# Sigmoids of the second merge in other batches, first squares on two engines, a root table asked for early, weight splits ahead of waiting rows

## The reference

```
first block:  h = rms_norm(x); proj = h @ w_in
              gated linear attention (4 heads, chunks of 64), a width-3 causal convolution branch
              merged = sigmoid(g_a)*y_a + sigmoid(g_c)*y_c;  x += merged @ w_out
              x += sigmoid(rms_norm(x) @ w_ple_gate) * (p @ w_ple_proj);  x = rms_norm(x)
second block: z = rms_norm(x) @ w_in_2
              y_a = mlstm(z) @ w_up_a       (4 heads, forward and backward, chunks of 128)
              y_b = diff_attention(z) @ w_up_b   (4 heads, softmax pairs, ALiBi bias)
              x += (sigmoid(z[gate 0])*y_a + sigmoid(z[gate 1])*y_b) @ w_out
              h2 = rms_norm(x); aff = softmax(h2 @ w_router)    (16 experts)
              each expert takes its 64 best tokens: silu(xe@w_gate)*(xe@w_up) @ w_down, times aff
              out = rms_norm(x + sum of the experts' rows)
```

## Time and profile before

| | |
|---|---|
| runs before | 1989.58, 1990.76, 1990.95 us, median 1990.76 |
| the profiled execution | 1988.47 us, span 1986.7 us |
| mean granted PE clock | 0.988 |
| PE busy | 1890.8 us (95%), 8735 matmuls |
| DVE / ACT / POOL busy | 728.8 / 520.7 / 68.8 us |
| DMA | 504.93 MB, 432 to 434 GB/s in nearly all of the second half |
| chain that ended last, by share | PE 66%, DMA 23%, issue 7%, ACT 2%, DVE 1%, POOL 1% |

### The profile page before, as it was taken

The page is one execution under the profiler, slowest core; times in us unless marked ns, Lnnn a source line. Parts: engine busy times, 40 slices in busy tenths (PEclk is TensorE's granted clock), DMA queues, the critical chain, the costliest instruction groups (busy, mean ns, idle before and its releaser), DMA issues.

```text
span 1986.7 us, 20688 instructions
## 1 busy us (share of the span) xinstructions
PE 1890.8 (95%) x8735; PEld 1147.6 (58%) x8735; DVE 728.8 (37%) x1213; ACT 520.7 (26%) x839; POOL 68.8 (3%) x62
## 2 busy tenths in 40 slices
PE   8999999999999999999997999999898998999998
PEld 6788888888887888876874333333233333333332
DVE  6544444333356764786353111111111110111112
ACT  5444323222345343277532000000000000000002
POOL 2000000000014001100020000000000000000000
PEclk9999999999999999999998999999999999999999
DMA  5221322322323232121377999999999999999997
GB/s 188 85 85 64 117 95 96 98 100 100 106 89 106 74 128 107 64 64 43 113 313 302 421 427 432 432 434 432 432 433 432 432 432 432 432 433 432 433 428 297
DMA packets 49324, 504.93 MB, mean 254 GB/s; under 512 B 6416, under 2 KB 7440, under 8 KB 30544
## 3 DMA queue, kind: packets, MB, share of 16 engines
q1 hardware_dynamic: 48368, 502.49, 62.0%
q10 hardware_dynamic: 864, 1.12, 0.2%
HBM read 499.39 MB, written 4.19 MB: 253 GB/s over the span
## 4 chain that ended last, share of the span: by engine, by line
PE 66%; DMA 23%; issue 7%; ACT 2%; DVE 1%; POOL 1%; SPq 0%; ACTq 0%; POOLq 0%; DVEq 0%
PE ps L2107 35%; DMA ring_a<-in_experts_in 22%; PE ps L2463 10%; PE ps L2474 6%; PE ps L2042 4%; PE ps L2422 3%; PE ps L2446 1%; PE ps L2509 1%; POOL xacc L785 1%; POOL gbl L819 0%; ACT hidT L1237 0%; DMA x_in<-in_xT_in 0%; PE ps L2485 0%; PE ps L2227 0%; PE ps L2210 0%
## 5 line engine op out<-in xcount | busy, mean ns | idle before, releaser
L2463 PE MATMUL ps<-ring_a,xe 128*64 128x512 f32 x1504 | 342.8, 609 | 43.6 <-DMA ring_a<-in_experts_in 43.0
L2463 PEld LDWEIGHTS ps<-ring_a,xe 128*64 128x64 f32 x1504 | 107.0, 140 | 273.3 <-issue 211.9
L1282 DVE TENSOR_TENSOR d_lo<-d_raw,d_hi 128x1024 fp32r<-128x1024 f32 x166 | 208.3, 1263 | 123.8 <-ACT d_hi L851 123.1
L2107 PE MATMUL ps<-n_hi,d_hi 128*128 128x512 f32 x448 | 176.0, 393 | 1.5 <-DVE d_lo L1282 0.8
L2107 PE MATMUL ps<-n_lo,d_hi 128*128 128x512 f32 x448 | 174.5, 389 | 0.0
L2107 PE MATMUL ps<-n_hi,d_lo 128*128 128x512 f32 x448 | 174.4, 389 | 0.0
L851 ACT ACTIVATE d_hi<-d_raw 128x1024 fp32r<-128x1024 f32 x166 | 170.9, 1049 | 9.3 <-DMA d_raw<-in_tiles_in 7.6
L1512 DVE TENSOR_TENSOR hid<-hid,ps 128x512 f32<-128x512 f32 x32 | 20.6, 683 | 411.8 <-PE ps L2463 385.4
L1950 DVE TENSOR_TENSOR acc<-acc,ps 128x1024 f32<-128x1024 f32 x56 | 64.6, 1214 | 242.6 <-PE ps L2446 242.6
L2474 PE MATMUL ps<-ring_a,hidT 128*64 128x512 f32 x648 | 145.7, 596 | 7.5 <-DMA ring_a<-in_experts_in 4.3
L2463 PE MATMUL ps<-ring_b,xe 128*64 128x512 f32 x464 | 103.1, 594 | 3.3 <-DMA ring_b<-in_experts_in 3.3
(11 more groups left out here) (503 smaller groups left out, 2730.2 us busy)
## 6 DMA issues: line engine op xcount, KB each, us to landing
ring_a<-in_experts_in SPq DMA_DIRECT2D x56, 4096.0 KB, 42.0
ring_b<-in_experts_in SPq DMA_DIRECT2D x28, 3072.0 KB, 42.5
d_raw<-in_tiles_in SPq DMA_DIRECT2D x166, 512.0 KB, 3.3
ring_a<-in_experts_in SPq DMA_DIRECT2D x31, 1024.0 KB, 13.0
ring_a<-in_experts_in SPq DMA_DIRECT2D x12, 2048.0 KB, 13.8
ring_b<-in_experts_in SPq DMA_DIRECT2D x5, 2048.0 KB, 13.9
ring_b<-in_experts_in SPq DMA_DIRECT2D x8, 1024.0 KB, 16.7
x_in<-in_xT_in SPq DMA_DIRECT2D x4, 512.0 KB, 6.8
```

The lines of the kernel that those rows point to most:

```text
L1282: dve.tensor_tensor(d_lo[:, n % SLOTS, :, :], d_raw[:, n % SLOTS, :, :], d_hi[:, n % SLOTS, :, :].bitcast(F32), ALU.subtract).then_inc(t_l ...
L2107: mm = pe.matmul(bank, lt[:, n, gr.k0 + k, :], rt[:, k, :], start=k == 0 and m == 0, stop=k == gr.nk - 1 and m == 2)
L2463: mm = pe.matmul(ps[half * CAP:(half + 1) * CAP, 2 * m + q, :], xe[:, k, :], slot(e, n)[:, (2 * q + half) * S:(2 * q + half + 1) * S], sta ...
```

## The change

Nothing of what is computed changes, except the order in which the first eight squares are added. There are five edits.

1. The sigmoids of g2a: n = 0, 1 go into `mlstm_norm` at ("g2a", 3), behind the sigmoid of `moT`; n = 2 to 7 stand in one batch at ("g2a", 7); the batch at ("ua", 2) is gone.
2. At ("g2b", 7) ACT splits the tile after `hd_hi` and before the eight sigmoids; before, it split it ahead of both.
3. In the ub groups ACT splits the tile first and then waits for the row of the merge.
4. POOL adds squares 0 to 3 only; DVE adds 4 to 7 and then both sums, between the early splits. PE waits for DVE.
5. The root table is asked for ahead of the wait for the logits, and the DMA of the triangle is issued behind the root.

```diff
@@ -491,8 +491,8 @@
         set_act = Steps(sem("setup_act"), ["warm", "root"])
         set_dve = Steps(sem("setup_dve"), ["gf2", "gks", "mgs"])
         u_act = Steps(sem("mix_act"), [f"hi{k}" for k in range(KD)] + [f"sq{k}" for k in range(KD)] + ["root"])
-        u_dve = Steps(sem("mix_dve"), [f"lo{k}" for k in range(KD)] + ["R"])
-        u_pool = Steps(sem("mix_pool"), [f"sum{k}" for k in range(1, KD)])
+        u_dve = Steps(sem("mix_dve"), [f"lo{k}" for k in range(KD)] + [f"sum{k}" for k in range(5, KD)] + ["sum", "R"])
+        u_pool = Steps(sem("mix_pool"), [f"sum{k}" for k in range(1, 4)])
         u_pe = Steps(sem("mix_pe"), ["sum"])
         h_dve = Steps(sem("normed_dve"), [n for k in range(KD) for n in (f"h{k}", f"lo{k}")])
         h_act = Steps(sem("normed_act"), [f"hi{k}" for k in range(KD)])
@@ -777,7 +777,7 @@
             pool.wait_ge(set_pool.sem, set_pool.count("reset1"))
             set_pool.done(pool.memset(reset[:, 0:S:GCH], 0.0), "reset")
 
-            for k in range(1, KD):
+            for k in range(1, 4):
                 pool.wait_ge(u_act.sem, u_act.count(f"sq{k}"))
                 if k > 1:
                     pool.wait_ge(u_pool.sem, u_pool.count(f"sum{k - 1}"))
@@ -926,6 +926,11 @@
                 act.wait_ge(mq_dve.sem, mq_dve.count("c4", n))
                 mq_act.done(act.activation(mqkT[:, n, :], scr[1 + n % 2][:, 0:S], ACT.Silu, bias=vcol("cb2", n)), "silu")
 
+            def splits(gr):
+                for n in range(len(TILES)):
+                    if SPLIT[n] == gr.g:
+                        split1(n)
+
             def after(gr):
                 name, i = gr.name, gr.i
                 if name == "gate":
@@ -1046,6 +1051,9 @@
                 biases(0)
                 read_done(act, "mo", MH - 1)
                 f_act.done(act.activation(moT[:, :, :], moT[:, :, :], ACT.Sigmoid), "sig")
+                for n in range(2):
+                    read_done(act, "g2a", n)
+                    sa_act.done(act.activation(graw[:, n, :], graw[:, n, :], ACT.Sigmoid), f"s{n}")
 
             def mlstm_out(h):
                 act.wait_ge(f_t.sem, f_t.count("t", h))
@@ -1160,12 +1168,12 @@
                         mlstm_out(k - FIRST_F)
                     if 0 <= k - FIRST_D < ND + 5:
                         attention(k - FIRST_D)
-                if (name, i) in (("g2a", KD - 1), ("ua", 2)):
-                    for n in range(4) if name == "g2a" else range(4, KD):
+                if (name, i) == ("g2a", KD - 1):
+                    for n in range(2, KD):
                         read_done(act, "g2a", n)
-                        x = graw[:, n, :] if n < 2 else glog(n)
-                        sa_act.done(act.activation(x, x, ACT.Sigmoid), f"s{n}")
+                        sa_act.done(act.activation(glog(n), glog(n), ACT.Sigmoid), f"s{n}")
                 elif (name, i) == ("g2b", KD - 1):
+                    splits(gr)
                     for n in range(KD):
                         read_done(act, "g2b", n)
                         sb_act.done(act.activation(gbl[:, n, :], gbl[:, n, :], ACT.Sigmoid), f"s{n}")
@@ -1190,10 +1198,11 @@
             act.wait_ge(set_pool.sem, set_pool.count("eps"))
             u_act.done(act.activation(R[:, :], ps[:, 7, :], ACT.Sqrt, bias=eps[:, :], scale=1.0 / D), "root")
             for gr in STREAM:
+                if gr.name == "ub":
+                    splits(gr)
                 evict(gr)
-                for n in range(len(TILES)):
-                    if SPLIT[n] == gr.g:
-                        split1(n)
+                if gr.name != "ub" and (gr.name, gr.i) != ("g2b", KD - 1):
+                    splits(gr)
                 if (gr.name, gr.i) == ("dq", 3):
                     gate_logs()
                 if gr.name in ("q", "k"):
@@ -1207,11 +1216,11 @@
                     p_act.done(act.activation(pT_hi[:, k, :], pT_raw[:, k, :], ACT.Copy), f"hi{k}")
                 chain(gr.name, gr.i)
 
-            act.wait_ge(t_dve.sem, t_dve.count("raw"))
-            act.dma_start(tri_raw[:, :], tri_in[:, :]).then_inc(s_tri, 16)
             act.wait_ge(set_act.sem, set_act.count("warm"))
             set_act.done(act.activation(warm[:, :], eps[:, :], ACT.Sqrt), "root")
+            act.wait_ge(t_dve.sem, t_dve.count("raw"))
             t_act.done(act.activation(esm[:, 4:8], lraw[:, :, NE], ACT.Sqrt, bias=eps[:, :], scale=1 / D), "root")
+            act.dma_start(tri_raw[:, :], tri_in[:, :]).then_inc(s_tri, 16)
             act.wait_ge(t_dve.sem, t_dve.count("lg"))
             t_act.done(act.activation(lg[:, :, :], lg[:, :, :], ACT.Exp), "exp")
             for t, b in enumerate((0, 4, 6, 0)):
@@ -1848,7 +1857,18 @@
                 dve.wait_ge(u_act.sem, u_act.count(f"hi{k}"))
                 u_dve.done(dve.scalar_tensor_tensor(out=u_lo[:, k, :], in0=x_in[:, k, :], scalar=vcol("mix", k),
                                                     in1=u_hi[:, k, :].bitcast(F32), op0=ALU.mult, op1=ALU.subtract), f"lo{k}")
-            for n in pre[1:]:
+            for n in pre[1:3]:
+                split1(n)
+            for k in range(5, KD):
+                dve.wait_ge(u_act.sem, u_act.count(f"sq{k}"))
+                if k > 5:
+                    dve.wait_ge(u_dve.sem, u_dve.count(f"sum{k - 1}"))
+                u_dve.done(dve.tensor_tensor(xsq[:, 4, :], xsq[:, 4, :], xsq[:, k, :], ALU.add), f"sum{k}")
+            for n in pre[3:]:
+                if n == pre[4]:
+                    dve.wait_ge(u_pool.sem, u_pool.count("sum3"))
+                    dve.wait_ge(u_dve.sem, u_dve.count(f"sum{KD - 1}"))
+                    u_dve.done(dve.tensor_tensor(xacc[:, :], xacc[:, :], xsq[:, 4, :], ALU.add), "sum")
                 split1(n)
             dve.wait_ge(s_table, 16)
             dve.wait_ge(u_pe.sem, u_pe.count("sum"))
@@ -2297,7 +2317,7 @@
 
             def chain(name, i):
                 if (name, i) == ("q", 2):
-                    pe.wait_ge(u_pool.sem, u_pool.count(f"sum{KD - 1}"))
+                    pe.wait_ge(u_dve.sem, u_dve.count("sum"))
                     u_pe.done(pe.matmul(ps[:, 7, :], ones[:, :], xacc[:, :], start=True, stop=True), "sum")
                 elif (name, i) == ("v", 0):
                     gates_wide()
```

## The result

The changed kernel takes 1977.82 us in the median (1977.08 to 1978.91, 6 runs) against 1989.06 (1988.4 to 1990.95, 6 runs) for the kernel before on the same chip: ratio 0.9944, 95% interval 0.9934 to 0.9954, or 11.2 us faster. The forecast was 1979.3, the sum of the terms -11.5.

A forecast was written before the change was run, and what follows sets the result against it. PE work up to the first expert-weight reload, then a fixed DMA stream, was taken to bound the kernel. Terms -1.9 - 5.7 - 2.3 - 1.6 = -11.5 us gave 1977.0 from the profile, 1979.3 against the median; range 1975.5 to 1984.5.

The forecast's parts named there:

- The bound: From the first expert-weight reload the DMA stream runs without pause; PE time won before it shortens the end one for one.
- Rival C: The end doesn't follow PE, the DMA stream keeps its own pace: no change, 1990.8 us; chance 0.03.
- Edit 4: At the start, PE's sum of squares no longer waits for POOL: -1.9 us, bounds -1.95 and -1.7.
- the slow case: At the start, DVE's additions stretched by half, as POOL's were: 1.05 us each instead of 0.69.
- Edit 1: In ua, waits shrink to 0.5 and 0.6 and PE keeps full rate: -5.7 us, bounds -6.8 and -2.7.
- A: In ua the clock falls all the same, costing 3.1 us: -8.4 in all, 1982.4 us; chance 0.12.
- D: In ua the batch of six sets off a row of half-rate steps: slower, 1994.8 us with five; chance 0.03.
- Edits 2 and 3: In ub and out2, the `hd_lo` wait and the 1.51 at out2 go: -2.3 us, bounds -2.6 and +0.5.
- walk through the groups: In ub, DVE reads bank 0 some 2.5 us before PE needs it; the last row comes 3 after out2 begins.
- Rival B: In ub, tile landings hold `m_hi`, so the moved splits give nothing or cost 0.5: 1982.1 us; chance 0.08.
- Edit 5: In routing, the root table loads during ACT's wait, so `lg` comes earlier: -1.6 us, bounds -2.0 and -1.2.
- The gather: Behind the routing, the clock's rise relative to the gather may shift: 0 in the sum, 1 us either way.

The follow-up runs named there:

- w4_busy8: Changed kernel with 8 matmuls of no use in PE's wait for the routing threshold; 1974.87 us, ratio 0.9925 to the kernel before.
- p3: Kernel before with only the first sum's additions shared between POOL and DVE; ratio 0.9989, timed 2.2 us faster.
- p1_batches: Kernel before with only the g2a sigmoids rebatched and the batch at ("ua", 2) gone; ratio 0.9972, timed 5.6 us faster.
- p2_ub: Kernel before with only ACT's tile splits moved, behind `hd_hi` and ahead of the merge rows in ub; ratio 0.9987, timed 2.6 us faster.
- v2_tri_late: Changed kernel with the triangle's DMA issued behind the exponentials; 1978.27 us, one run.
- N = 7: Changed kernel with 7 matmuls of no use in PE's wait for the routing threshold; 1976.98 us, ratio 0.9938 to the kernel before.

## Why the prediction was right

**The bound.** The end is the first reload plus a fixed amount of bytes: the reload moved by 11.15 and the span by 11.2; with the eight matmuls by 14.43 and 15.1. Rival C is out. That the first pair agrees so closely is luck: from the first reload to the end it takes 896.7 to 898.5 us in the 14 profiles, 897.4 in both of this pair.

**Edit 4**, -1.9: -1.72 in the profile, in an execution whose first matmul began 0.46 later (7.44 against 6.98) and which came to the last matmul of ("q", 2) 0.33 later. From there to the row behind the sum it takes 2.74 before and 0.68 both after and in p3: the edit is worth 2.06, 1.95 of waiting and 0.11 in the sum matmul itself. DVE's three additions took 1.13 each (3.38 / 3), above the slow case of 1.05, and the split behind them 1.22 instead of 1.87; the two misses nearly cancel, and PE's asking at 25.99 covered both.

**Edit 1**, -5.7: -6.04, with waits of 0.28 and 0.53 where 0.5 and 0.6 were forecast, and the full rate kept. Its split in waits and clock was shown by filling the wait: 2.78 of clock, against 3.06 read from the rows. What the prediction did not see is that the clock's part varies between executions, 1.6 to 2.8. So the edit is worth on average less than the profile before says: 3.3 of waits (6.04 - 2.78) and 2.1 of clock, the mean of the five profiles that keep waits and idling, 5.3 in all by this estimate; that 6.04 came out near 5.7 is in part the luck of a dear case. The isolated run, 5.6 in the times (3.4 to 7.8), can't tell the two. Rivals A and D (the clock falls anyway, once or in a row) did not occur in any of the seven profiles with the block gone. But one argument against A was weak: the wait at the start, which had left the clock at full rate before, was followed by the fall in `p1_batches`.

**Edits 2 and 3**, -2.3: -2.44, and -2.67 alone. The two waits account for it when taken from start to start: the first matmul of each group came 0.87 and 1.90 behind its predecessor instead of 0.23, that is 2.31, where the rows' idle time gives 1.98, since an idle time is counted from the modelled end. (What `p2_ub` shows beyond the 2.44 is not accounted for.) The other 0.13 of the 2.44 is nearly all at the last row, k = 7, for which PE waited shortly before too: there a start comes 0.51 behind its predecessor before and 0.40 after. The prediction had put this at 0.3. Its walk through the groups was too kind in two places: DVE had read ub 6's bank 0.33 ahead of PE, not 2.5, and the last `m_lo` ended 4.9 behind the start of out2 (1007.25 - 1002.38), not 3. The wait is gone, but by a third of a microsecond. Rival B is out: no row shows `m_hi` held by a landing.

**Edit 5**, -1.6: -1.70. Two errors nearly cancel: from root to `lg` the forecast took 1.74 (1063.96 to 1065.7), with 0.34 for the DMA's issue and almost nothing for the root; measured are 1.67, with 0.06 for the issue and 0.32 for the root (1053.98 to the load at 1054.30 in `v2_tri_late`, where no issue stands between).

**The gather**, 0 with 1 either way: +0.75. The sign could not be known from the profile of before; that the clock is what it turns on was right, and all 14 first gathers lie between 3.65 (no fall) and 6.65. Those with the fall took 5.08 to 6.65, so against the 5.21 of before this step could have come out anywhere from -0.1 to +1.4.

The sum, -11.5 against -11.15, owes a part of its closeness to errors that cancel (-0.34 in ua, -0.14 in ub and -0.10 at the root against +0.18 at the start and +0.75 in the gather). The forecast of 1979.3 lies 1.5 above the time, since the median of the first three runs before (1990.76) is 1.7 above that of the six runs that the result goes by.

## What to carry to other kernels

Read the granted clock beside every wait of a few microseconds: here waits of 3.8 in all on PE cost 1.6 to 2.8 more behind them, and with the longer one filled nothing more. Read it in more than one execution, since the same wait has several prices. A short wait that falls in front of a busy stretch is worth filling if the filler can be made to end just ahead of the event, and worth leaving if it can't: eight matmuls gained 3.0 us, seven nothing that could be told, fourteen lost 3.6. And when one edit takes work from an engine, follow its consumer: what it saves in an earlier wait, it asks for sooner at the next.

## What the runs showed of the hardware that I had not expected

- A float32 matmul of 512 columns with weights of 128 columns takes 0.87 us (12.18 / 14). The gather's, with 64, come to 0.45 each (3.65 / 8) because they run in pairs: two write the two halves of the partitions of one bank, their records start at most 0.04 us apart, the next two 0.43 later, and one record lasts 0.59 us as for 128 columns (`w4_busy8`, granted clock 1.00). No run shows what one alone would take.
- The same wait in the same program is followed by half rate in some executions only: that of 1.43 to 1.90 at the start in one of seven, that of 1.7 to 1.8 near 633 in two of 14.
- In one execution (N = 7) the clock fell behind idling of 1.13 and 0.61 us: the three short matmuls at 1065.49, ahead of the idling of 1.08, already take 0.74 us, against 0.45 with N = 8, where 0.26, 0.61 and 1.08 were followed by no fall. One profile of each, so this is an observation and no bound.
- An ACT table load can be hidden in a wait: it stands directly in front of the first activation of its set, so with a tiny activation of that set written ahead of the wait it ran from 1052.04 to 1053.32, while the logits came at 1053.7. The activation behind it started 0.01 us later.
- A DMA issued by ACT behind an activation ran beside that activation: its 0.33 us cost 0.06.
